# The two products that turn the one-hot matrix: behind the down products, or spread inside their second half

## The reference, cut to what matters

```python
def body(acc, blk):
    tok_b, w_b, e = blk                                # the tokens of one expert, their weights
    xb = xpad[tok_b]                                   # gather
    hb = jax.nn.silu(xb @ w1[e]) * (xb @ w3[e])        # "up": 1024 -> 256, twice
    yb = (hb @ w2[e]).astype(jnp.float32) * w_b[:, None]   # "down": 256 -> 1024
    return acc.at[tok_b].add(yb), None                 # scatter
```

## Time and profile before

| | before |
|---|---|
| median of 3 runs | 1410.54 us |
| profiled execution, its own time | 1415.53 us |
| its span | 1413.8 us |
| TensorE busy (PE) | 1344.6 us, 95% |
| VectorE busy (DVE) | 382.3 us, 27% |
| ScalarE busy (ACT) | 359.5 us, 25% |
| moved from and to HBM | 506.20 MB, mean 358 GB/s |
| granted TensorE clock over the span | 0.978 |

### The profile page before, as it was taken

One profiled execution on the slowest core, in us unless ns is written; L12 is line 12 of the kernel. 1 busy time (PEld: TensorE's weight loads), 2 busy tenths in 40 slices (PEclk: granted clock), 3 DMA queues, 4 the chain that ended last, 5 costly groups with the idle time before them and its releaser, 6 DMA issues.

```text
span 1413.8 us, 17675 instructions
## 1 busy us (share of the span) xinstructions
PE 1344.6 (95%) x6640; PEld 697.1 (49%) x6640; DVE 382.3 (27%) x1158; ACT 359.5 (25%) x642; POOL 7.2 (1%) x32
## 2 busy tenths in 40 slices
PE   4998998999999999999987998999999999999996
PEld 1865455444445445445454746444544444444443
DVE  1494152221211222221122416122222222222113
ACT  2035032222222222222222113222222222222222
POOL 1000000000000000000000000000000000000000
PEclk9999989999999999999997999999999999999998
DMA  9997575999999999999879009599999999999981
GB/s 368 397 408 313 222 299 233 417 407 420 418 416 409 422 411 410 417 417 421 329 302 391 29 32 410 240 410 410 420 421 409 415 416 421 414 407 414 418 339 50
DMA packets 79799, 506.20 MB, mean 358 GB/s; under 512 B 8072, under 2 KB 9224, under 8 KB 23440
## 3 DMA queue, kind: packets, MB, share of 16 engines
q1 hardware_dynamic: 78880, 504.13, 87.1%
q10 hardware_dynamic: 880, 1.52, 0.3%
HBM read 504.57 MB, written 1.05 MB: 358 GB/s over the span
## 4 chain that ended last, share of the span: by engine, by line
PE 89%; DVE 6%; ACT 2%; DMA 2%; issue 1%; DVEq 0%; SPq 0%; ACTq 0%
PE PS L1201 33%; PE PS L1233 16%; PE PS L1184 10%; PE PS L1244 9%; PE PS L1171 4%; PE PS L1150 4%; DVE gates L994 3%; PE PS L1296 2%; PE PS L1218 2%; DMA ring<-in_ada_w 2%; PE PS L1114 2%; PE PS L1254 2%; PE PS L1210 1%; PE PS L1326 1%; ACT hT L524 1%
## 5 line engine op out<-in xcount | busy, mean ns | idle before, releaser
L1201 PE MATMUL PS<-ring,xn 128*64 128x512 f32 x1120 | 250.0, 599 | 1.9 <-ACT xn L612 1.9
L1233 PE MATMUL PS<-ring,hidT 128*64 128x512 f32 x1072 | 244.8, 598 | 2.6 <-DVE hidT L907 2.6
L1201 PE MATMUL PS<-ring,xg 128*64 128x512 f32 x1024 | 226.8, 595 | 0.0
L1201 PEld LDWEIGHTS PS<-ring,xn 128*64 128x64 f32 x1120 | 78.1, 138 | 145.7 <-issue 143.2
L1184 PE MATMUL PS<-hot,xh 128*128 128x256 f32 x512 | 142.0, 310 | 6.4 <-DVE hot L878 4.8
L1201 PEld LDWEIGHTS PS<-ring,xg 128*64 128x64 f32 x1024 | 70.7, 137 | 130.2 <-issue 127.9
L1233 PEld LDWEIGHTS PS<-ring,hidT 128*64 128x64 f32 x1072 | 71.0, 136 | 126.7 <-issue 114.8
L1184 PE MATMUL PS<-hot,xl 128*128 128x256 f32 x512 | 127.4, 281 | 0.0
L1184 PEld LDWEIGHTS PS<-hot,xh 128*128 128x128 f32 x512 | 97.5, 190 | 57.3 <-issue 49.2
L618 ACT ACTIVATE hid<-PS 128x256 f32<-128x256 f32 x67 | 25.8, 385 | 355.0 <-PE PS L1201 355.0
L1244 PE MATMUL PS<-yh,hotT 128*128 128x512 f32 x268 | 108.4, 405 | 0.0
(11 more groups left out here) (201 smaller groups left out, 1001.8 us busy)
## 6 DMA issues: line engine op xcount, KB each, us to landing
ring<-in_moe_w SPq DMA_DIRECT2D x402, 1024.0 KB, 10.5
ring<-in_ada_w SPq DMA_DIRECT2D x48, 1024.0 KB, 13.9
ring<-in_ev_w_in SPq DMA_DIRECT2D x10, 1024.0 KB, 15.7
ring<-in_sh_w SPq DMA_DIRECT2D x6, 1024.0 KB, 8.7
ring<-in_ev_w_out SPq DMA_DIRECT2D x4, 1024.0 KB, 11.7
ring<-in_od_w_in SPq DMA_DIRECT2D x4, 1024.0 KB, 16.5
ring<-in_od_w_out SPq DMA_DIRECT2D x4, 1024.0 KB, 11.1
x<-in_x SPq DMA_DIRECT2D x1, 1024.0 KB, 5.4
```

Source lines behind the costliest of these rows:

```text
L1201: ins = M(PS[rows, 6, :], xg[gp][:, k, tokens], w13[:, :, k, :], start=(k == 0), stop=(k == KD - 1))
L1233: ins = M(PS[rows, 4 + h, :], hidT[:, j, rows], slot_view(slots[2][0], 2)[:, j, h * 512:(h + 1) * 512], start=(j == 0), stop=(j == 1))
```

## The change

`pair` no longer calls `down` and then `turn`; it calls a new function, `down_and_turn`. The first half of the down products (`h` = 0) is as it was. In the second half, each part `j` has one of the two turning matmuls in front of it: chunk 0 before `j` = 0, chunk 1 before `j` = 1. The waits of `turn` move with chunk 0, into the middle of the down products. `turn_filled` is raised by the matmul of chunk 1, `down_filled` by the last down matmul, which is now the last instruction. The "more" loop keeps `down` and `turn`.

```diff
+            def down_and_turn(f, experts, hidden_at, n, gather_at, hot_at=None):
+
+                pe.wait_ge(f.hidT_taken, hidden_at)
+                for slots in experts:
+                    pe.wait_ge(slots[2][1], slots[2][2])
+                for h in range(2):
+                    for j in range(2):
+                        if h:
+                            c, o = j, (n % 2) * P
+                            if c == 0:
+                                if hot_at is not None:
+                                    pe.wait_ge(f.hot_ready, hot_at)
+                                pe.wait_ge(f.gather_taken, gather_at)
+                            ins = M(PS[:, 7, c * HB:c * HB + TW], hot[:, n // 2, c, o:o + P], idw[:, n % 2, c, 0:TW],
+                                    start=True, stop=True)
+                            if c == TC - 1:
+                                ins.then_inc(f.turn_filled, 1)
+                        for hf, slots in enumerate(experts):
+                            rows = slice(hf * BLK, (hf + 1) * BLK)
+                            ins = M(PS[rows, 4 + h, :], hidT[:, j, rows],
+                                    slot_view(slots[2][0], 2)[:, j, h * 512:(h + 1) * 512],
+                                    start=(j == 0), stop=(j == 1))
+                ins.then_inc(f.down_filled, 1)
...
                     if first:
                         pe.wait_ge(ctl_ready, l + 1)
-                    down(f, experts, pr + 1)
-                    if not gathers:
-                        pe.wait_ge(f.hot_ready, pr + 3)
-                    turn(f, n, 2 * PAIRS + 2 if last else pr * 2 + 6 if gathers else 2 * PAIRS)
+                    down_and_turn(f, experts, pr + 1, n, 2 * PAIRS + 2 if last else pr * 2 + 6 if gathers else 2 * PAIRS,
+                                  None if gathers else pr + 3)
```

## The result

The changed kernel takes 1433.26 us (median of 4 runs, 1431.47 to 1435.05) against 1410.61 us (4 runs). The ratio is 1.0132, 95% interval 1.0107 to 1.0156. That is 18.6 us more by the ratio, where 19.8 us were worked out; 1433 lies in the range of 1423 to 1437. The profiled executions differ by 17.2 us (1432.76 against 1415.53 us), the spans by as much (1431.0 against 1413.8 us). So at a clock of 0.978 the change costs 17 to 19 us.

What follows compares the result with a forecast made beforehand. TensorE was taken as the bound. Per pair, two single turns (0.84 us) less 0.53 us saved behind down add 0.31 us; 64 times is 19.8 us on 1410.5, so 1430 us, range 1423 to 1437.

Steps and rivals of the forecast that it cites:

- The bound: TensorE bounds the kernel, 15.16 us per pair; what is added to its sequence in a pair is paid 64 times.
- The base: Time the added 19.8 us is put on: median 1410.5 us, 5 us below the profiled execution's 1415.5.
- 0.53 us out behind down: Between down and up, the turn's removal saves 0.53 us per pair, as up follows in the same half-width form.
- Two single turns at 0.42 us: Inside down, each turning matmul alone costs 0.42 us, two 0.84; net 0.31 us more per pair.
- the fixed part: Price of one change to full width and back: 0.31 us from the whole pair, 0.36 from the "more" loop.
- 64 times: 64 turns stand behind down with an idle weight side before them; 64 x 0.31 = 19.8 us.
- The moved wait: Wait for ScalarE, now inside down, costs nothing: 0.74 us to spare, 0.2 in the last pair of a layer.
- Rival A: Each single turn inside down costs a whole 0.53 us, 33.9 us more, 1444; chance 0.08.
- Rival B: Turning weight loads hide behind streaming half-width steps inside down; 19 us less, 1391; chance 0.04.
- Rival C: No change: drains overlap with something already paid, or a change gets cheaper; 1410.5 within 3 us; chance 0.04.
- The ceiling on a gain: DMA needs 14.87 us per pair at 423 GB/s, so any gain stops at 0.30 us a pair.

Runs made afterwards that it cites:

- experiment 7: Kernel before the change, with the turn moved ahead of down, right behind the second gather, into bank 5: ratio 0.9851, 1396.01 us.
- experiment 2: Changed kernel with the turning matmul of chunk 1 written twice in a row: ratio 1.0188 to the kernel before.
- experiment 3: Changed kernel with the turning matmul of chunk 1 done a second time behind the last down matmul: ratio 1.0312 to the kernel before.
- experiment 4: Changed kernel with each turning matmul written as two of half width, read as float32, at the same places: ratio 0.9964 to the kernel before.
- experiment 8: The kernel of experiment 7 without the low parts in gather, four matmuls per call for eight: ratio 0.978 to the kernel before.
- experiment 6: Changed kernel with its full-width turning matmuls read as float32, nothing else: ratio 1.0281 to the kernel before.

## Why the prediction was right, point by point

- **The bound.** TensorE's sequence, with no wait that lasts. Right: 0.30 us more per pair came through as time, 64 times, and so did 0.34 us less (experiment 7).
- **The base.** Wrong, and small: the sum was put on 1410.5 us, since the median was 5 us below the profiled execution and "the difference is the same in both". In the changed kernel it isn't: the profiled execution took 1432.76 us, where 1435.3 was forecast, and the median is 0.5 us above it. So the forecast of 1430 is 3.3 us below the median, while the forecast for the profiled execution is 2.5 us above what it took. The 5 us fit the spread with the granted clock (see the result) and aren't a property of the kernel; that both errors are small beside the range was luck in part.
- **0.53 us out behind down.** Right: up's loads follow in the beat of down.
- **Two single turns at 0.42 us.** Measured 0.41; net 0.30 us per pair for the forecast 0.31. Of the two values for the fixed part, 0.31 us from the earlier trace rows and 0.36 us with the earlier trace rows, the first is nearer for this change: 0.30 from experiment 2, 0.31 from experiment 3 less experiment 2. Experiment 7, which puts the turn between full matmuls as the earlier trace rows has it, saved 0.34, nearer to 0.36.
- **64 times.** 128 idle stretches for 64, 0.81 us each. By the periods, 64 x 0.30 = 19.2 us. The spans differ by 17.2 us; the chain places the rest outside the pairs. In the first layer, from the first up to the last residual sum, the chain grew by 9.7 us (534.8 to 544.5), in the second, from the first up to that of the "more" trip, by 9.5 us (484.9 to 494.5), together 19.3. The part ahead of the first pair was 1.1 us shorter (first up at 233.30 against 234.44), the part between the layers 0.8 longer, and the tail behind the last of those ups 1.7 shorter (32.8 against 34.5). In all three the same matmuls took another time, where the granted clock was lower in one execution or the other. Ahead of the first pair, where the two kernels do the same, 64 matmuls of the shared expert (L1296, L1320 in the changed kernel) took 13.88 us at a granted clock of 1.00 against 15.47 at 0.90; between the layers that line took 15.79 us at 0.88 against 13.87 at 1.00, and L1150 27.91 us at 1.00 against 29.59 at 0.94; in the tail the last scatter took 1.93 us at a clock of 1.00 against 3.48 at 0.52, near the 1.2 GHz level. Nothing points at the change there.
- **The moved wait.** 0.74 us to spare by the prediction, and 0.74 us by the trace (414.91 to 415.65). In the last pairs, too, the load that has the wait shows the same 0.81 us.
- **Rival A** (a whole 0.53 us per turn) would have given a period of 15.69 us and fell to the 15.46. **Rival B** (hidden between half-width steps) is false for full width, and the place where it would have been true is experiment 4: in one form the turn costs only its own instructions. **Rival C** (no price) fell to the result and to experiment 3.
- **The ceiling on a gain.** Right in kind: the DMA's 14.87 us proved to be 14.91. But "the DMA's 14.87 us stops it at 0.30" was too strict: experiment 7 saved 0.34 us a pair without a wait, on the lead that experiment 8 shows.

The Trainium skill's rule from "TensorEngine Tiling (Array Packing)", Key Properties, that a change of the mode drains TensorE, holds here with a price: 0.30 us per change and back, with 0.10 us from the last half-width step to the full load and about 0.20 us from the start of the last full matmul to the half-width load. What the Trainium skill says in "TensorE: Matmul & The Clock Gate", "Architectural detail: the array is 16× 32×32, not 1× 128×128", of weight loads pulled ahead shows here inside one form only: 0.14 us loads beside the streaming steps, but before all 128 turning loads the 0.81 us without one.

## What to carry to other kernels

Where TensorE is the bound, order its work by the form of the stationary operand: each change of form and back had a fixed price here, 0.30 us with one matmul or two between, so small products belong next to others of their form, or are rewritten in the form around them. To see it, look not at the busy share, which read 20.00 of 20.00 us in the windows with either kernel, but at idle stretches of the weight loads longer than the beat (0.81 against 0.29 us), and count them. And before a saving is booked, work out the next bound from bytes per period: here the DMA leaves room for one such saving and no more. Compare runs at the same granted clock: it moved this kernel by up to 10 us, half of what the change did.

## What the runs showed that was not expected

- The turn's two instructions cost 0.17 us between full matmuls, as the earlier trace rows has it and the expectation of experiment 7 overlooked, less than the 2 x 0.11 us that they have inside an excursion; so moving the turn saved 0.34 us and not 0.31.
- In float32, splitting a product into two half-width ones costs nothing: the 128 x 132 product takes 0.23 us as four half-width instructions (experiment 4), and at full width 0.41 + 0.16 - 0.30 = 0.27 us even with the change of form taken off (experiment 6). Against float32r at full width it does cost: 0.11 us per product there, so the half-width turn gained only 0.08 us a pair (15.16 to 15.08), where the turn ahead of down gained 0.34.
- The releaser that the profile names for an idle stretch was twice one that had been done 0.1 to 0.7 us earlier, on an instruction whose pause had another cause.
